# Second norm of a two-layer hybrid backbone stored in natural feature order, the mixture-of-experts gather reading every eighth column

## What is computed

```python
hc = modulate(rms_norm(xc, norm2_g[l]), mc[3], mc[4])    # h * (1 + scale) + shift
hs = modulate(rms_norm(xs, norm2_g[l]), ms[3], ms[4])
xc = xc + mc[5] * hier_moe(hc, *moe_args)
...
# hier_moe: top-1 of 4 groups, then top-2 of 8 experts inside it
act = silu(einsum('td,edf->tef', x, w_gate)) * einsum('td,edf->tef', x, w_up)
act = act * combine[..., None]
y = einsum('tef,efd->td', act, w_down)
```

## Time and profile before

| | us |
|---|---|
| three runs | 1051.6, 1052.5, 1057.79 |
| median | 1052.5 |
| profiled execution | 1051.57 |
| its span, first to last instruction | 1049.6 |
| TensorE busy in the span | 910.0 (87%) |
| VectorE busy in the span | 308.7 (29%) |
| mean granted TensorE clock | 0.944 of full speed |

### The profile page before, as it was taken

How to read it: one execution, slowest core, us unless ns; L and a number is a source line. 1 busy time by engine, 2 the same in 40 slices (tenths; PEclk the granted TensorE clock), 3 DMA queues, 4 the chain that set the end, 5 groups by cost and what they waited for, 6 DMA issues and landing times.

```text
span 1049.6 us, 14213 instructions
## 1 busy us (share of the span) xinstructions
PE 910.0 (87%) x5967; PEld 520.5 (50%) x5967; DVE 308.7 (29%) x762; ACT 200.9 (19%) x372; POOL 40.8 (4%) x74
## 2 busy tenths in 40 slices
PE   1799999979699777997699999999996997779963
PEld 0586556664565444564244444444446654445531
DVE  1120234831732111110277713332017321111103
ACT  3111112340211000100340005545002111001102
POOL 3000000111000000000000002100000000000000
PEclk9899999999799988998899999999996999989988
DMA  9999745999497999999944467144844979999993
GB/s 313 401 357 369 305 170 218 409 413 401 155 411 312 421 420 421 421 421 415 392 149 158 163 224 267 71 158 177 345 160 155 412 297 422 420 422 419 422 417 142
DMA packets 73414, 329.17 MB, mean 314 GB/s; under 512 B 5868, under 2 KB 6244, under 8 KB 49540
## 3 DMA queue, kind: packets, MB, share of 16 engines
q1 hardware_dynamic: 67380, 310.30, 74.4%
q0 software_dynamic: 5360, 16.49, 4.3%
q10 hardware_dynamic: 608, 1.44, 0.4%
HBM read 322.11 MB, written 6.09 MB: 313 GB/s over the span
## 4 chain that ended last, share of the span: by engine, by line
PE 69%; DMA 22%; DVE 3%; SPq 3%; ACT 2%; issue 1%; DVEq 0%
PE PS L724 67%; DMA ring<-in_moe_w_down 11%; DMA ring<-in_mod_w 5%; DMA ring<-in_moe_w_gate 5%; SPq L608 1%; SPq L619 1%; ACT scratch L1374 0%; ACT HT L1381 0%; SPq L615 0%; DVE H L1771 0%; DVE X L1766 0%; PE PS L757 0%; DVE scratch L1965 0%; PE PS L1313 0%; PE PS L1054 0%
## 5 line engine op out<-in xcount | busy, mean ns | idle before, releaser
L724 PE MATMUL PS<-ring,scratch 128*32 128x256 f32 (+3 forms) x2592 | 296.1, 464 | 63.6 <-DMA ring<-in_moe_w_gate 37.2
L724 PEld LDWEIGHTS PS<-ring,scratch 128*32 128x32 f32 (+2 forms) x2592 | 142.0, 128 | 211.5 <-issue 164.7
L724 PE MATMUL PS<-ring,HT 128*128 128x512 f32 x432 | 192.1, 598 | 2.7 <-ACT HT L1381 1.9
L724 PEld LDWEIGHTS PS<-ring,HT 128*128 128x128 f32 x432 | 81.4, 192 | 99.2 <-issue 95.5
L724 PE MATMUL PS<-scratch 128*128 128x512 f32 (+3 forms) x504 | 125.6, 434 | 3.5 <-DVE scratch L2419 1.8
L724 PEld LDWEIGHTS PS<-scratch 128*128 128x128 f32 (+2 forms) x504 | 60.4, 184 | 62.8 <-issue 54.8
L724 PE MATMUL PS<-scratch,H 128*128 128x128 f32 x640 | 84.7, 289 | 3.1 <-DVE scratch L2135 3.1
L724 PEld LDWEIGHTS PS<-scratch,H 128*128 128x128 f32 x640 | 79.6, 203 | 10.5 <-issue 10.5
L2239 DVE TENSOR_TENSOR scratch<-PS,scratch 128x256 f32<-128x256 f32 x20 | 8.5, 425 | 257.4 <-ACT scratch L1559 257.4
L724 PE MATMUL PS<-ring,cpad 128*32 128x256 f32 x768 | 49.3, 408 | 20.1 <-DMA ring<-in_mod_w 20.1
L1559 ACT ACTIVATE scratch<-PS 128x256 f32<-128x256 f32 x20 | 7.7, 384 | 253.8 <-PE PS L724 253.8
(11 more groups left out here) (295 smaller groups left out, 698.0 us busy)
## 6 DMA issues: line engine op xcount, KB each, us to landing
ring<-in_moe_w_up SPq DMA_DIRECT2D x64, 1024.0 KB, 19.0
ring<-in_moe_w_gate SPq DMA_DIRECT2D x56, 1024.0 KB, 17.7
ring<-in_moe_w_down SPq DMA_DIRECT2D x56, 1024.0 KB, 17.9
ring<-in_mod_w SPq DMA_DIRECT2D x24, 2048.0 KB, 15.7
ring<-in_odd_w_in SPq DMA_DIRECT2D x12, 2048.0 KB, 13.0
ring<-in_even_w_in SPq DMA_DIRECT2D x7, 2048.0 KB, 16.0
ring<-in_moe_w_down SPq DMA_DIRECT2D x16, 512.0 KB, 17.5
ring<-in_odd_w_out SPq DMA_DIRECT2D x4, 2048.0 KB, 7.6
```

Source lines behind the costliest of these rows:

```text
L724: return nc.tensor.matmul(out, lhsT, rhs, start=start, stop=stop, skip_group_check=True, **kw)
```

## The change

`H` gets two more views: `HN`, the 1024 features of a stream in natural order, and `HK`, the same memory seen as eight tiles whose columns lie eight words (32 bytes) apart. `scale_h` and `shift_h` write and read through `HN`; both gathers take their stationary operand through `HK`. No instruction, wait or transfer is added or taken away.

```diff
         H = sb("H", [P, S, KT, P])
+        HN = H[:, :, :, :].rearrange("t s k p -> t s (k p)")
+        HK = HN.rearrange("t s (p k) -> t s k p", k=KT)
...
-                            mm = matmul(PS[:, 4 + half, P * k:P * k + P], H[:, s, 4 * half + k, :],
+                            mm = matmul(PS[:, 4 + half, P * k:P * k + P], HK[:, s, 4 * half + k, :],
                                         SEL[:, par, s, :], s == 0, s == S - 1)
...
-                        mm = matmul(PS[:, 4 + half, P * k:P * k + P], H[:, s, 4 * half + k, :], SEL[:, 0, s, :],
+                        mm = matmul(PS[:, 4 + half, P * k:P * k + P], HK[:, s, 4 * half + k, :], SEL[:, 0, s, :],
                                     s == 0 and k == 0, s == S - 1)
...
-                st.mark(V.scalar_tensor_tensor(out=H[:, s, :, :].rearrange("t k p -> t p k"),
-                                               in0=X[:, s, :].rearrange("t (p k) -> t p k", k=KT), scalar=rstd[:, s:s + 1],
-                                               in1=GAIN[:, s, :].rearrange("t (p k) -> t p k", k=KT),
+                st.mark(V.scalar_tensor_tensor(out=HN[:, s, :],
+                                               in0=X[:, s, :], scalar=rstd[:, s:s + 1],
+                                               in1=GAIN[:, s, :],
                                                op0=ALU.mult, op1=ALU.mult))
...
-                h = H[:, s, :, :].rearrange("t k p -> t p k")
-                V.tensor_tensor(h, h, SHIFT[:, s, :].rearrange("t (p k) -> t p k", k=KT), ALU.add).then_inc(h_ready, 1)
+                h = HN[:, s, :]
+                V.tensor_tensor(h, h, SHIFT[:, s, :], ALU.add).then_inc(h_ready, 1)
```

## The result

The changed kernel takes 1078.9 us (median of 4 runs, 1076.9 to 1079.2) against 1055.1 us for the kernel before in the same comparison: a ratio of 1.0234, with a 95% interval of 1.0209 to 1.0259. It is slower by 22 to 27 us.

A forecast was written before the change was run, and what follows sets the result against it. Two limits alternate in the expert stages: TensorE up to the end of the DMA dip, DMA transfers behind it. Terms of 10.8 us in layer 0 and 10.2 in layer 1, 21.0 on 1051.6, gave 1072.6 us, range 1066 to 1080.

The forecast's parts named there:

- its own case: Whole kernel: stepped gather loads grow by 120 ns, paid mainly ahead of the dip's end; 1066 to 1080 us, chance 0.60.
- the dip's end: Expert stages, DMA back at full rate from 338 us: TensorE delays ahead shift everything, later ones only if queued loads run dry.
- VectorE's saving is covered: Scaling of stream 1 ends 0.7 us earlier, but prefix matmuls hold the copy: at most 0.05 us a layer, counted as nothing.
- The load: TensorE's gather weight load: 120 ns more, about 312 for 192, setting a pace of 238 ns; 3.8 us more a step.
- 1.75 ns a place: Memory under gather loads: one place handed out in 1.75 ns, taken from VectorE's stepped write; 224 ns for 128 columns.
- 53 + 59 = 112 ns for 64 pairs of words: Transposes at L1059, loading every second word: their column time also comes out at 1.75 ns a place.
- rival 1: Gather loads: the step is hidden, loads stay at 192 to 201 ns, no slower, 1051.6 us; chance 0.22.
- First gather, steps 0 and 1: Gathers ahead of step 2: first gather +1.5 us in layer 0, +0.9 in layer 1; steps 0 and 1 +7.7 each layer.
- Step 2's down loads: Step 2's gather delays its down matmuls and the next down loads: 3.8 less 2.2 us spare, +1.6.
- Steps 6 to 8: Late gathers without TensorE idle time: the ring covers them, 7.7 of 9.6 us spare used in layer 0; nothing paid.
- Rival 2, the clock: Gathers of steps 0, 1 and 2: clock drops to 0.50, following bursts pay 2.55 us each, 15.3 more, 1087.9; chance 0.10.

The follow-up runs named there:

- VectorE's half alone: Against the kernel before, scale and shift write 1024 neighbouring words while gathers load neighbouring words as before: 1053.0 us against 1054.1, ratio 0.9998.
- the middle kernel: Against the kernel before, only the gathers of steps 2 to 5 (8 of 20) load every eighth word: ratio 1.0016.
- The kernel with late gathers alone: Against the kernel before, only the gathers of steps 6 to 8 (6 of 20) load every eighth word: ratio 1.0030.

## Why the prediction came out right, point by point

It forecast +21.0 us, 1066 to 1080 for its own case; the profiled execution shows +27.6, the comparison +24.6 (2.34% of 1051.6). The mechanism holds: a load that sets TensorE's pace, paid ahead of the dip's end and mostly hidden behind it. Of the load's price one reason failed, and one term put at nothing was not nothing.

**VectorE's saving is covered.** Right: a wait of 0.68 us took its place, in the changed kernel as in VectorE's half alone:

```profile
278.30 0.32 DVE L2084 COPY scratch<-PS 128x160 f32<-128x160 f32 x1 [0.68 <-PE PS L727]
```

**The load.** Forecast 120 ns more, 312 in all and a pace of 238 ns; measured 143, 335 and 244. The pace, which is what TensorE pays, came nearer than the record of the load. The stair between two and four words, which the prediction had only assumed, is shown by the runs. But of the two reasons for 1.75 ns a place, the second, 53 + 59 = 112 ns for 64 pairs of words, failed. The gather's load of every second word costs 4 ns more and not 59. And the transposes of every second word (L1059), whose records are 59 ns longer than those of neighbouring words (L1054), hardly cost TensorE more in the kernel before. Behind the transposes that start at 316.18 in the earlier trace rows stand:

```profile
316.39 0.40 PE L1059 MATMUL PS<-const,scratch 128*128 128x128 f32 x2
316.63 1.95 PE L724 MATMUL PS<-scratch,H 128*128 128x128 f32 x16
```

From start to start two of them take 0.24 us, and two of L1054 0.21. The length of a load's record is thus not its price. The changed kernel shows it a second time: its transposes of neighbouring words, whose loads were not changed, have records of 140 to 273 ns behind stepped loads, where they had 140 to 144.

```profile
L1057 PEld LDWEIGHTS PS<-const,scratch x40: 140/205/273, 289.5 to 1031.6; 128*128 128x128 f32 x40
```

What is left is VectorE's price for words written alone: another engine, and a write. No run shows that the two engines pay for the same thing. That its 1.75 ns came near TensorE's 244 / 128 = 1.9 ns a column is in part luck.

By the Trainium skill (SBUF — State Buffer, section Door 1: The DMA port swizzle) lines of 16 bytes give the full rate from two hits a line on. The gather nearly agrees: two words from 16 bytes cost it 4 ns, one word 120 to 143. The 201 ns that the prediction held against this rule are the record and not the pace. The Trainium skill's rule in rival 1 (TensorE: Matmul & The Clock Gate, section LDWEIGHTS), a time by the columns alone, fails: the same 128 columns take 192 to 335 ns.

**First gather, steps 0 and 1.** Forecast +1.5 and +0.9, and +7.7 in each layer. The chain gives 7.88 - 6.06 = 1.8 and 7.89 - 6.66 = 1.2, and 4.0 us for a gather, 8.1 for two. In the changed kernel's SP the up loads behind the dip go out 10.1 us later than in the earlier trace rows:

```profile
343.13 2.03 SPq L622 DMA_DIRECT2D ring<-in_moe_w_up  x4
354.96 2.32 SPq L622 DMA_DIRECT2D ring<-in_moe_w_down  x4
...
469.38 12.83 SPq L622 DMA_DIRECT2D ring<-in_moe_w_down  x4
```

**Step 2's down loads.** They are issued at 354.96 for 340.83, 14.1 us later, 4.0 more than the up loads, against a spare time put at 2.2: the forecast was +1.6, and the middle kernel's lost transfer of 2.0 us is about that. The changed kernel loses (81 + 46) x 6 / 421 = 1.8 us in layer 0 and 130 x 6 / 421 = 1.9 in layer 1:

```profile
350.00:356.00 6.00, 6.00 (x62) 2.98 (x65) 3.34 (x10) 0.60 (x1) 0.00 (x0) 1.00 0.87 340
356.00:362.00 6.00, 6.00 (x56) 2.70 (x52) 0.00 (x0) 0.00 (x0) 0.00 (x0) 1.00 0.94 375
...
890.00:896.00 6.00, 6.00 (x92) 2.71 (x84) 2.54 (x9) 0.60 (x1) 0.00 (x0) 1.00 0.80 291
```

**Steps 6 to 8, the term that failed.** The prediction let TensorE begin step 6 when its gate lands. It came later. In the changed kernel step 5 is already behind (its waits for gates in this stage are down to 3.8 us), and step 6's gate begins within a burst that starts at 430.29 with 3.6 us of down matmuls, so at 433.9: 12.5 us after the 421.4 of before, where the loads were to come 10.8 later. With two gathers of 4.0 us this uses up just more than the 9.6 us that were spare. The last of the next lap's six slots is issued at 469.38 + 12.83 = 482.2, and DMA drops (changed kernel, layer 0 and then layer 1):

```profile
476.00:482.00 6.00, 6.00 (x39) 3.01 (x42) 3.33 (x10) 0.60 (x1) 0.00 (x0) 1.00 0.89 367
482.00:488.00 6.00, 6.00 (x60) 3.06 (x53) 0.00 (x0) 0.00 (x0) 0.00 (x0) 1.00 1.00 369
488.00:494.00 6.00, 6.00 (x84) 4.06 (x83) 0.20 (x1) 0.00 (x0) 0.00 (x0) 1.00 0.99 399
...
506.00:512.00 6.00, 3.54 (x64) 1.70 (x56) 0.00 (x0) 0.53 (x1) 0.00 (x0) 1.00 0.94 320
...
1016.00:1022.00 6.00, 6.00 (x74) 2.86 (x71) 0.76 (x2) 0.60 (x1) 0.00 (x0) 1.00 1.02 410
1022.00:1028.00 6.00, 6.00 (x71) 2.91 (x70) 0.00 (x0) 0.19 (x1) 0.00 (x0) 1.00 1.00 389
```

That is (54 + 52 + 22) x 6 / 421 = 1.8 us in layer 0. From 506 to 512, behind step 8's gather, another 101 x 6 / 421 = 1.4 us are lost. In layer 1, which was forecast to have more to spare, it is (11 + 32) x 6 / 421 = 0.6. The kernel with late gathers alone, 0.30%, points the same way; "nothing" should have been some 3 to 4 us. By the count of slots the last load is late by far less than 1.8 us; why the rate drops so early is open.

Together: 3.0 us in the first gathers (forecast 2.4), 16.2 in steps 0 and 1 (15.4), 3.7 in step 2 (3.2) and 3.8 in steps 6 to 8 (nothing). That is 26.7 of the 26.8 us. The last two are estimates from lost transfer, so that the sum comes out so close is partly chance.

**The ends.** In layer 0 the last scatter started 511.02 and starts 525.75, 14.7 later, in layer 1 25.9. But layer 0's took 5.78 us before (granted clock 0.64 from 511 to 517) and takes 3.67 now (1.00 from 525.75 to 529), and layer 1's the other way round (1.00 from 1031 to 1037, now 0.68 from 1056 to 1062). This moves 2 us from one layer to the other and cancels; the stages of 12.7 and 14.1 us are to be read with it.

**Rival 2, the clock.** It doesn't fall: it is 1.00 through steps 0 to 3, with half as many matmuls in a gather's time as before. The mean over the run rose from 0.944 to 0.963 while TensorE's waits shrank; from 356 to 374 us, where it had waited 6.31 us for a gate, the clock was 0.81 and is 1.00.

## What to carry to other kernels

Let the operand that is read often lie as its reader wants it, and pay for the odd layout where it is written: eight stepped writes cost 5.7 us of a VectorE that waited anyway; with 640 stepped loads TensorE is busy for 67 us more. Read the price of a load from start to start, not from the length of its record. When a part of a kernel alternates between two limits, price an extra microsecond by its place: ahead of the point where the transfers reach their full rate it is paid in full, in the waits behind that it costs little until they are used up, and slack that was counted with the old arrival times has to be counted again with the new ones. Before a shortened instruction is booked as a gain, look for a second wait that ends level with it.

## What was not expected

The price of a stepped load is a stair and not a slope: 192 and 196 ns for columns 4 and 8 bytes apart, 329 and 335 for 16 and 32. At 64 bytes it falls again, to 312. A load of neighbouring words that nobody changed has a record of up to 273 ns for 144 when it stands behind stepped ones. VectorE reads runs of two and of four words at the rate of neighbouring words, 1.04 to 1.05 ns a word.
